# Expert passes of at most 96 rows by strip groups alone, with their slots in reverse, and strip groups behind both row halves in every pass

## The chip, the cores and the metric

One core of one Trainium2 chip runs the whole kernel as one program. The metric is the device time in microseconds of one execution; lower is better. The time before is the median of three runs, 1945.91 us.

## The reference

The kernel computes one residual block for 1024 tokens of width 1024 in float32: a convolution group and a windowed attention group, their output projection, and then a mixture of experts. Only the last part is touched by the change:

```
logits = xf @ router_w + router_b           # 32 experts
top_val, top_idx = lax.top_k(logits, 4)     # 4 experts for each token
gates = softmax(top_val)
h = xb @ w1[e] + b1[e]                      # 1024 -> 2048, rows of one expert
x_glu = minimum(h[:, :1024], 7.0)
x_lin = clip(h[:, 1024:], -7.0, 7.0)
act = x_glu * sigmoid(1.702 * x_glu) * (x_lin + 1.0)
y = act @ w2[e] + b2[e]                     # 1024 -> 1024
out[token] += gate * y
```

Counted from the reference's own routing of its own inputs, the 32 experts get 187, 176, 173, 150, 149, 149, 144, 139, 139, 138, 137, 132, 130 and 129 tokens (14 experts with more than 128), 15 experts get 103 to 128, and three get few: expert 17 gets 77, expert 25 gets 95 and expert 27 gets 75. Expert 0 gets 121.

## The kernel before, in words

The mixed part (convolution, attention, projection, routing) fills the first 425 us. Then follows a loop of passes, one for each expert here, in which the engines run their own loops and meet by semaphores.

**What a pass is.** A pass has 256 slots. The tokens of the expert fill slots 0, 1, 2 and so on, in the order of their ranks (`prep` subtracts a base from the ranks, `one_hots` makes a one-hot matrix of them, `slots_to_tokens` turns it into token numbers on TensorE). The slots behind them get tokens that did not choose the expert, whose gate is exactly 0. All 256 slots are gathered in every pass.

**Tiers.** Each pass is computed for a width n out of `WIDTHS`, the smallest that holds its tokens. The passes are sorted by width, cyclically from the tier of expert 0, by small operations on VectorE just before the loop. Here that gives 18 passes with n = 128, then 3 with 136, 5 with 144, 3 with 152, 2 with 176 and 1 with 192, which is the last.

**TensorE in a pass (`pe_pass`).** The first product has eight blocks m, each of two sides and eight k: 128 matmuls of a 128x128 piece of `w1_sb` (stationary) against n columns of `xT`. The profile shows each float32 matmul as two instructions, so a pass has 256. Block m waits for `hid_free`, the first also for `xt_ev`, the transposed rows: a pass with n = 128 waits for the first half of the slots only (`q4_low`). The second product has slots 0 to 127 as stationary operand, eight pieces for each half of the 1024 columns (`down_rows`, 16 matmuls with 512 columns, 32 instructions), and, in passes of more than 128 rows, the other slots in groups of 32 (`down_quads`). A group uses the array as four strips of 32 columns: each strip takes the same 32 slots against another quarter of the output columns, so a group is 8 x 4 matmuls of 256 columns, 64 instructions. The order is first row half, strip groups, second row half.

**The other engines in a pass.** VectorE adds the bias and clips (`hidden_a`), multiplies (`hidden_b`), ScalarE makes the sigmoid. GpSimd issues eight indirect gathers of the next pass' rows, two behind each of the blocks 4 to 7 of the first product (`gather_quads`), and then the indirect adds of the finished rows into the output (`add_quads` four times where the pass is wide, then `add_rows`); at the head of the next pass it waits until all of these have landed. VectorE transposes the gathered rows into `xT` (eight transposes) when all eight gathers have landed, which fires `xt_ev`; then it adds b2 to what ScalarE has copied out of PSUM: first row half, four strip groups, second row half. The strip groups are copied and biased in every pass, used or not.

**The weights.** There is one buffer for `w1` and one for `w2`. SyncE's loop issues for the next pass: each half of w1 (two transfers of 2048 KB) when blocks 3 and 7 of the first product are done, the first half of w2 (2048 KB) when the first row half and the strip groups are done, the second when the second row half is done, then b2.

```
            if n == P:
                pe.sem_inc(yq_mm, QUADS)
            else:
                down_quads(-(-(n - P) // QG_ROWS))
```

Of the kernel before, what the change touches and what calls it, by code (L numbers as in the profile page):

```python
# [18 lines left out]
P = 128  # L19
# [14 lines left out]
WIDTHS = [128, 136, 144, 152, 176, 192, 256]  # L34
QG_ROWS = 32
# [11 lines left out]
def hybrid_block(nc, x, norm1_g, w_in, conv_w, conv_b, conv_ln_g, conv_ln_b, q_norm_g, k_norm_g, sinks,  # L47
# [11 lines left out]
    with ExitStack() as ctx:  # L59
# [115 lines left out]
        given = sb("given", [P, P])  # L175
        least = sb("least", [P, P])
# [124 lines left out]
        def _(sp):  # L301
# [69 lines left out]
            with sp.Fori(1, n_pass) as q:  # L371
# [61 lines left out]
        def _(pool):  # L433
# [95 lines left out]
            with pool.Fori(0, n_pass) as q:  # L529
# [7 lines left out]
                q_quads = pool.snap(q * QUADS)  # L537
                with pool.If(over > 0):
# [11 lines left out]
        def act_pass(a, q):  # L550
# [22 lines left out]
            take_rows(0)  # L573
            take_quads()
            take_rows(1)
# [241 lines left out]
        def dve_pass(v, q, e, e_next, prep, one_hots):  # L817
# [80 lines left out]
            add_b2(0)  # L898
            q_quads = v.snap(q * QUADS + QUADS)
# [4 lines left out]
            add_b2(1).then_inc(y_ready, 1)  # L904

        @block.vector
        def _(v):
# [43 lines left out]
            link(v.tensor_scalar(tc[:, 1:2], qcol[:], tc[:, 0:1], float(SLOTS // NE), ALU.subtract, ALU.mult))  # L951
# [186 lines left out]
            def prep(ranks, base):  # L1138
                return v.tensor_scalar(r8[:], ranks, base, None, ALU.subtract)
# [23 lines left out]
            link(v.tensor_scalar(tier, left, float(WIDTHS[0]), None, ALU.is_gt))  # L1163
            for n in WIDTHS[1:-1]:
# [5 lines left out]
            link(v.tensor_scalar(keys, circ, 0.0, float(len(WIDTHS)), ALU.is_lt, ALU.mult))  # L1170
# [12 lines left out]
            link(v.tensor_scalar(t1(TIER), t1(WRAP), float(len(WIDTHS)), -float(len(WIDTHS)), ALU.is_ge, ALU.mult))  # L1183
            link(v.tensor_tensor(t1(TIER), t1(TIER), t1(WRAP), ALU.add))
            link(v.tensor_scalar(place[:], iota_c[:, 0:TQ], t1(AT), None, ALU.is_equal))
# [11 lines left out]
            v.tensor_copy(baseB[:], bank[1][:, 3 * TQ:4 * TQ])  # L1197
# [18 lines left out]
        def pe_pass(pe, q, n, halves, slots_to_tokens):  # L1216
# [4 lines left out]
            for m in range(MT):  # L1221
# [12 lines left out]
                if m == 1:  # L1234
                    slots_to_tokens(q + 2, halves)
# [449 lines left out]
```

## Time and profile before

| | |
|---|---|
| median of 3 runs | 1945.91 us (1942.98 to 1947.94) |
| the profiled execution's own time | 1941.44 us |
| its span, first to last instruction | 1939.6 us |
| TensorE (PE) busy | 1904.7 us, 98% of the span |
| weight loads (PEld) busy | 1442.8 us, 74% |
| VectorE (DVE) busy | 1023.9 us, 53% |
| mean granted TensorE clock | 0.996 |
| moved by DMA | 517.28 MB, mean 267 GB/s |

Everything is counted from one profiled execution, in microseconds from the start of its span. PE is TensorE's matmuls, PEld its weight loads, which run beside matmuls, DVE is VectorE, ACT ScalarE, POOL GpSimd, SPq the queue of SyncE. L1230 is line 1230 of the kernel before. A row of a timeline is a group of like instructions: start, time to the end of the last, engine, line, operation, and in brackets the idle time before it and what ended it. The ends of matmuls are modelled, so lengths here are taken from start to start.

### The profile page before, as it was taken

Reading aid. Unit: us, or ns where it says so; the run is one execution under the profiler, and the core shown is the slowest. Engines: PE = TensorE matmul, PEld = TensorE weight load, DVE = VectorE, ACT = ScalarE, POOL = GpSimd, SP = SyncE. Lnnn points to the kernel's source line nnn. Section 1 sums busy time; section 2 is a strip of 40 time slices with the busy share of each in tenths; the row PEclk is TensorE's granted clock in tenths of the full one; section 3 lists DMA queues with packets and bytes.
Section 4 is the critical chain, followed back from the end, with each engine's and each line's share of the span. In section 5 each row is a group of like instructions: output and inputs, shape, how many; then the busy total and the mean of one; then the engine's idle time right before and its main releaser. Section 6 shows DMA issues by size and latency. Waiting matters only on the chain.

```text
span 1939.6 us, 34852 instructions
## 1 busy us (share of the span) xinstructions
PE 1904.7 (98%) x12360; PEld 1442.8 (74%) x12361; DVE 1023.9 (53%) x2829; ACT 439.3 (23%) x966; POOL 455.7 (23%) x434
## 2 busy tenths in 40 slices
PE   8999999989999999999999999999999999999997
PEld 5555554468887778888877888888888888888874
DVE  5999973365555455555545555444444444443332
ACT  4367583121111111111111111111111111110110
POOL 3110110011222112112221211333333333322223
PEclk9999999999999999999999999999999999999999
DMA  7000226358999999999999999999999998887762
GB/s 249 1 1 1 71 60 247 107 184 309 347 354 339 354 354 353 346 338 355 350 343 354 354 348 348 321 319 319 319 319 317 310 311 307 300 299 262 235 215 47
DMA packets 248770, 517.28 MB, mean 267 GB/s; under 512 B 13265, under 2 KB 29165, under 8 KB 248720
## 3 DMA queue, kind: packets, MB, share of 16 engines
q1 hardware_dynamic: 223392, 453.50, 64.8%
q0 software_dynamic: 25312, 63.08, 12.5%
q8 instruction: 35, 0.57, 0.1%
q14 instruction: 15, 0.12, 0.0%
q10 hardware_dynamic: 16, 0.00, 0.0%
HBM read 483.49 MB, written 33.05 MB: 266 GB/s over the span
## 4 chain that ended last, share of the span: by engine, by line
PE 93%; DVE 4%; ACT 1%; DMA 1%; issue 1%; POOL 1%; POOLq 0%; DVEq 0%
PE bank L1230 51%; PE bank L1247 23%; PE bank L1445 6%; PE bank L1321 4%; PE bank L1261 3%; DVE arena L974 2%; PE bank L1357 2%; PE bank L1367 1%; PE bank L1395 1%; PE bank L1615 0%; PE bank L1419 0%; PE bank L1548 0%; PE bank L1404 0%; POOL rs L445 0%; DMA arena<-token_rows,idx_next 0%
## 5 line engine op out<-in xcount | busy, mean ns | idle before, releaser
L1230 PE MATMUL bank<-arena 128*128 128x128 f32 (+5 forms) x8192 | 997.8, 283 | 2.0 <-issue 2.0
L1230 PEld LDWEIGHTS bank<-arena 128*128 128x128 f32 x8192 | 985.9, 191 | 16.9 <-issue 16.9
L1247 PE MATMUL bank<-arena 128*128 128x512 f32 x1024 | 448.5, 594 | 0.0
L419 POOL DMA_INDIRECT arena<-token_rows,idx_q x256 | 248.4, 970 | 709.9 <-PE bank L1230 661.2
L1247 PEld LDWEIGHTS bank<-arena 128*128 128x128 f32 x1024 | 191.2, 190 | 228.7 <-issue 228.7
L835 DVE TENSOR_SCALAR arena<-bank,b1c 128x256 f32<-128x256 f32 x256 | 123.5, 483 | 402.0 <-PE bank L1230 393.4
L556 ACT ACTIVATE arena<-arena 128x256 f32<-128x256 f32 x256 | 106.7, 417 | 860.4 <-DVE arena L835 860.4
L883 DVE STREAM_TRANSPOSE arena<-arena 128x256 f32<-128x256 f32 x256 | 87.3, 408 | 196.9 <-DMA arena<-token_rows,idx_q 196.9
L974 DVE SCALAR_TENSOR_TENSOR arena<-arena,cols 128x512 f32<-128x512 f32 (+1 forms) x226 | 182.3, 807 | 12.8 <-ACT arena L622 5.8
L428 POOL DMA_INDIRECT out<-arena,idxq_cur x56 | 91.3, 1631 | 165.8 <-DVE arena L902 153.3
L847 DVE SCALAR_TENSOR_TENSOR arena<-arena 128x256 f32<-128x256 f32 x256 | 108.8, 425 | 38.0 <-DVE arena L844 9.9
L564 ACT ACTIVATE arena<-bank,gate_cur 128x512 f32<-128x512 f32 x64 | 44.0, 687 | 352.4 <-PE bank L1247 352.4
L837 DVE TENSOR_SCALAR arena<-bank,b1c 128x256 f32<-128x256 f32 x256 | 121.5, 474 | 0.0
L1445 PE MATMUL bank<-arena 128*128 128x512 f32 x256 | 115.6, 599 | 0.8 <-ACT arena L693 0.8
L1321 PE MATMUL bank<-arena 128*128 128x512 f32 x256 | 113.2, 595 | 0.3 <-DVE arena L925 0.3
L844 DVE TENSOR_TENSOR arena<-arena 128x256 f32<-128x256 f32 x256 | 107.3, 419 | 2.9
L424 POOL DMA_INDIRECT out<-arena,idx_cur x32 | 51.3, 1603 | 241.3 <-DVE arena L896 237.6
L896 DVE SCALAR_TENSOR_TENSOR arena<-arena,gate_cur 128x512 f32<-128x512 f32 x64 | 48.1, 752 | 86.1 <-ACT arena L564 74.9
L1321 PEld LDWEIGHTS bank<-arena 128*128 128x128 f32 x256 | 47.5, 190 | 55.0 <-issue 54.6
L1445 PEld LDWEIGHTS bank<-arena 128*128 128x128 f32 x256 | 46.8, 190 | 52.7 <-issue 52.6
L444 POOL TENSOR_SCALAR ss<-ss 128x1 f32<-128x1 f32 (+1 forms) x24 | 10.0, 417 | 271.4 <-DVE ss L987 156.1
L1261 PE MATMUL bank<-arena 128*32 128x256 f32 x1088 | 61.6, 380 | 0.0
(235 smaller groups left out, 1103.6 us busy)
## 6 DMA issues: line engine op xcount, KB each, us to landing
arena<-in_w SPq DMA_DIRECT2D x192, 2048.0 KB, 13.7
arena<-in_b SPq DMA_DIRECT2D x32, 512.0 KB, 13.3
arena<-in_x SPq DMA_DIRECT2D x16, 512.0 KB, 5.4
token_rows<-arena SPq DMA_DIRECT2D x8, 576.0 KB, 3.2
out<-arena SPq DMA_DIRECT2D x8, 512.0 KB, 5.7
arena<-in_b SPq DMA_DIRECT2D x128, 32.0 KB, 11.9
arena<-token_rows,idx_q POOLq DMA_INDIRECT x256
arena<-in_w_in SPq DMA_DIRECT2D x2, 1536.0 KB, 10.8
```

The source lines that it names most:

```text
L419: pool.indirect_dma_start(out=gath_q[:, g, :], out_offset=None, in_=quads_d, in_offset=bass.IndirectOffsetOnAxis(ap=idx_q[:, g:g + 1], axis=0)
L556: a.activation(sg[:, m % 2, :], g1[:, m % 2, :], ACT.Sigmoid, scale=ALPHA).then_inc(sg_ready, 1)
L835: v.tensor_scalar(g1[:, r, :], bank[r][:, 0:SLOTS], b1c[:, m:m + 1], LIMIT, ALU.add, ALU.min).then_inc(g1_ready, 1)
L837: v.tensor_scalar(l1[:, r, :], bank[r][:, SLOTS:], b1c[:, MT + m:MT + m + 1], LIMIT + 1.0, ALU.add, ALU.min).then_inc(hid_free, 1)
L844: v.tensor_tensor(tt[:, r, :], g1[:, r, :], sg[:, r, :], ALU.mult).then_inc(dve_loop, 1)
L847: v.scalar_tensor_tensor(act[:, m, :], l1[:, r, :], 1.0 - LIMIT, tt[:, r, :], ALU.max, ALU.mult).then_inc(act_ready, 1)
L974: link(v.scalar_tensor_tensor(out_, zT[:, c, lo + j:lo + j + n], col(CW + c * WIDTH + j), out_, ALU.mult, ALU.add))
L1230: last = mm(bank[m % 2][:, side * SLOTS:side * SLOTS + n], w1_sb[:, k, lo:lo + P], xT[:, k, 0:n], start=k == 0, stop=k == KD - 1)
L1247: last = mm(bank[4 + b][:], act[:, m, 0:P], w2_sb[:, m, b * HALF:(b + 1) * HALF], start=m == 0, stop=m == MT - 1)
L1261: last = mm(dst[j * QG_ROWS:(j + 1) * QG_ROWS, at:at + D // 4], act[:, m, lo:lo + QG_ROWS], w2_sb[:, m, j * (D // 4):(j + 1) * (D // 4)], ...
L1321: last = mm(dst[:], w_cv[:, k, lo:lo + P], uT[:, k, h * HALF:(h + 1) * HALF], start=k == 0, stop=k == KD - 1)
L1445: last = mm(bank[mixed_bank(t) + b][:], src, w_o[:, k, b * HALF:(b + 1) * HALF], start=part_ == 0 and i == 0, stop=part_ == 1 and i == CT - 1)
```

## The change

- A new tier `FEW`: a pass of at most 96 rows (but for expert 0's) is computed with n = 96. It sorts behind 256, so the three such passes come last, behind the one of 192.
- In these passes the slots are reversed: rank r goes to slot 255 - r. `prep` multiplies by a sign of the pass (`turned`), and the base table carries the flag. The rows then stand in slots 160 to 255: the first product takes `xT[:, k, 160:256]`, the second product runs strip groups 1, 2 and 3 alone, and no row half. Such a pass waits for the transposes of all slots, and both parts of w2.
- In all passes the strip groups follow both row halves: on TensorE, ScalarE, VectorE (add of b2) and GpSimd (the adds into the output). Both halves of w2 wait for the strip groups, and the load of b2 for VectorE's last strip group.
- `hidden_a(0)` moves ahead of `prep` and `one_hots` on VectorE, and `slots_to_tokens` from behind block 1 to behind block 2.
- Passes with n = 96 find the tokens of both slot halves (16 small matmul instructions), those with n = 128 mostly those of one.

```diff
+FEW = 96
+FOLD = 2048
+TIERS = len(WIDTHS) + 1
...
                 for c in range(2):
                     sp.wait_ge(yt_mm, q * 2 + (c - 1))
-                    if c == 0:
-                        sp.wait_ge(yq_mm, q * QUADS)
+                    sp.wait_ge(yq_mm, q * QUADS)
                     load_w2(sp, c, e)
                 sp.wait_ge(y_ready, q)
+                sp.wait_ge(yq_ready, q * QUADS)
                 load_b2(sp, e)
...
+                pool.wait_ge(y_ready, q + 1)
+                pool.sem_inc(pool_past, 1)
+                add_rows(pool)
                 with pool.If(over > 0):
                     for g in range(QUADS):
                         pool.wait_ge(yq_ready, q_quads + g + 1)
                         pool.sem_inc(pool_past, 1)
                         add_quads(pool, g)
                     pool.reg_add(wide, wide, 1)
-                pool.wait_ge(y_ready, q + 1)
-                pool.sem_inc(pool_past, 1)
-                add_rows(pool)
...
             take_rows(0)
+            take_rows(1)
             take_quads()
-            take_rows(1)
...
-            link(prep(rank[:, :, ds(e_next, 1)].rearrange("p t o -> p (t o)"), baseB[:, ds(q + 1, 1)]))
+            hidden_a(0)
+            link(prep(rank[:, :, ds(e_next, 1)].rearrange("p t o -> p (t o)"), baseB[:, ds(q + 1, 1)],
+                      turned[:, ds(q + 1, 1)]))
             one_hots()
-            hidden_a(0)
...
             add_b2(0)
+            add_b2(1).then_inc(y_ready, 1)
             q_quads = v.snap(q * QUADS + QUADS)
             for g in range(QUADS):
...
-            add_b2(1).then_inc(y_ready, 1)
...
-                return v.tensor_scalar(r8[:], ranks, base, None, ALU.subtract)
+                return v.tensor_scalar(r8[:], ranks, base, sign, ALU.subtract, ALU.mult)
...
+            link(v.tensor_scalar(turned[:], bank[1][:, 3 * TQ:4 * TQ], 0.0, None, ALU.is_gt))
+            link(v.tensor_scalar(baseB[:], bank[1][:, 3 * TQ:4 * TQ], -float(FOLD), None, ALU.mult))
+            link(v.scalar_tensor_tensor(baseB[:], turned[:], float(FOLD + SLOTS - 1), baseB[:], ALU.mult, ALU.add))
+            link(v.tensor_scalar(turned[:], turned[:], -2.0, 1.0, ALU.mult, ALU.add))
             v.sem_inc(hid_free, 2)
...
+            at = SLOTS - n if n < P else 0
...
-                            pe.wait_ge(xt_ev, q4 if n > P else q4_low)
-                        last = mm(bank[m % 2][:, side * SLOTS:side * SLOTS + n],
-                                  w1_sb[:, k, lo:lo + P], xT[:, k, 0:n],
+                            pe.wait_ge(xt_ev, q4_low if n == P else q4)
+                        last = mm(bank[m % 2][:, side * SLOTS + at:side * SLOTS + at + n],
+                                  w1_sb[:, k, lo:lo + P], xT[:, k, at:at + n],
                                   start=k == 0, stop=k == KD - 1)
                 last.then_inc(hid_mm, 1)
-                if m == 1:
+                if m == 2:
                     slots_to_tokens(q + 2, halves)
...
-            down_rows(0)
             if n == P:
                 pe.sem_inc(yq_mm, QUADS)
+            if n >= P:
+                down_rows(0)
+                down_rows(1)
             else:
-                down_quads(-(-(n - P) // QG_ROWS))
-            down_rows(1)
+                pe.wait_ge(w2_in[0], q16)
+                pe.sem_inc(yt_mm, 2)
+            if n != P:
+                down_quads(range((SLOTS - n) // QG_ROWS - QUADS, QUADS) if n < P else range(-(-(n - P) // QG_ROWS)))
...
-                for i, n in enumerate(WIDTHS):
+                for i, n in enumerate(WIDTHS + [FEW]):
```

On TensorE, the second product of a pass of 136 rows before (L1230 is the first product, L1247 a row half, L1261 a strip group):

```order
L1230 MATMUL bank<-arena 128x136 x16
L1242 ISA
L1243 REGISTER_ALU
L1247 MATMUL bank<-arena 128x512 x8
L1261 MATMUL bank<-arena 32x256 x32
L1247 MATMUL bank<-arena 128x512 x8
```

And a pass of the new tier on TensorE in the changed kernel (L1241 is the first product, L1276 a strip group; no row half is left):

```order
L1241 MATMUL bank<-arena 128x96 x16
L1286 ISA
L1276 MATMUL bank<-arena 32x256 x32
L1269 REGISTER_ALU
L1276 MATMUL bank<-arena 32x256 x32
L1269 REGISTER_ALU
L1276 MATMUL bank<-arena 32x256 x32
```

Between blocks of the first product and the three strip groups stands nothing else; in the passes of 128 rows and more both L1258 row halves now stand together, with the strip groups behind them.

On GpSimd, the end of the loop before (L419 gathers, L428 adds of strip groups, L424 adds of row halves):

```order
L419 DMA arena<-token_rows,idx_q 128x288 x2
L538 COMPARE_AND_BRANCH
L540 ISA
L428 DMA out<-arena,idxq_cur 4096x256
L540 REGISTER_ALU
L428 DMA out<-arena,idxq_cur 4096x256
L540 REGISTER_ALU
L428 DMA out<-arena,idxq_cur 4096x256
L540 REGISTER_ALU
L428 DMA out<-arena,idxq_cur 4096x256
L543 REGISTER_ALU
L424 DMA out<-arena,idx_cur 1024x1024
```

And in the changed kernel:

```order
L423 DMA arena<-token_rows,idx_q 128x288 x2
L428 DMA out<-arena,idx_cur 1024x1024
L545 COMPARE_AND_BRANCH
L547 ISA
L432 DMA out<-arena,idxq_cur 4096x256
L547 REGISTER_ALU
L432 DMA out<-arena,idxq_cur 4096x256
```

The add of the rows (512 KB) now goes first, and the four adds of strip groups come last; a pass of the new tier issues all five.

## Rows read from the trace of the kernel before

**Rows 1.** The page: busy time of each engine, and the chain that ended last by line.

```profile
PE 1904.7 (98%) x12360; PEld 1442.8 (74%) x12361; DVE 1023.9 (53%) x2829; ACT 439.3 (23%) x966; POOL 455.7 (23%) x434
PE bank L1230 51%; PE bank L1247 23%; PE bank L1445 6%; PE bank L1321 4%; PE bank L1261 3%; DVE arena L974 2%; PE bank L1357 2%; PE bank L1367 1%; PE bank L1395 1%; PE bank L1615 0%; PE bank L1419 0%; PE bank L1548 0%; PE bank L1404 0%; POOL rs L445 0%; DMA arena<-token_rows,idx_next 0%
```

**Rows 2.** Windows, one pass each (128, 128, 144 rows): length, busy times, clock, DMA share, GB/s.

```profile
597.43:640.26 42.83, 42.83 (x299) 35.16 (x298) 23.08 (x74) 7.45 (x15) 9.26 (x9) 1.00 0.99 348
1154.20:1197.23 43.03, 43.03 (x307) 35.36 (x306) 22.00 (x69) 7.45 (x15) 9.26 (x9) 1.00 0.98 347
1340.88:1390.48 49.60, 49.60 (x372) 40.02 (x371) 22.48 (x70) 7.56 (x15) 16.21 (x14) 1.00 0.92 313
```

**Rows 3.** Timeline of PE, a pass of 128 rows: last four blocks, then second product.

```profile
612.15 14.54 PE L1230 MATMUL bank<-arena 128*128 128x128 f32 x128
626.53 13.90 PE L1247 MATMUL bank<-arena 128*128 128x512 f32 x32
```

**Rows 4.** Timeline of PE, wide passes of 136, 152 and 176 rows.

```profile
1212.68 15.07 PE L1230 MATMUL bank<-arena 128*128 128x136 f32 x128
1227.59 7.03 PE L1247 MATMUL bank<-arena 128*128 128x512 f32 x16
1234.55 3.66 PE L1261 MATMUL bank<-arena 128*32 128x256 f32 x64
...
1606.00 16.78 PE L1230 MATMUL bank<-arena 128*128 128x152 f32 x128
1622.62 7.03 PE L1247 MATMUL bank<-arena 128*128 128x512 f32 x16
...
1788.59 7.11 PE L1261 MATMUL bank<-arena 128*32 128x256 f32 x128
```

**Rows 5.** Timeline of PEld: weight loads whose matmuls have one column.

```profile
286.85 0.86 PEld L1470 LDWEIGHTS bank<-ones_ln,arena 128*128 128x128 f32 x7 [0.24 <-issue]
```

**Rows 6.** Timelines of POOL, DVE and PE: last gather of a pass, then the transposes.

```profile
628.84 0.95 POOL L419 DMA_INDIRECT arena<-token_rows,idx_q  x1 [0.30 <-issue]
...
634.95 2.73 DVE L883 STREAM_TRANSPOSE arena<-arena 128x256 f32<-128x256 f32 x8 [6.15 <-DMA arena<-token_rows,idx_q]
...
1781.63 7.03 PE L1247 MATMUL bank<-arena 128*128 128x512 f32 x16
1791.10 2.73 DVE L883 STREAM_TRANSPOSE arena<-arena 128x256 f32<-128x256 f32 x8 [7.30 <-DMA arena<-token_rows,idx_q]
```

**Rows 7.** The queue of SyncE (w2 L290, w1 L285), and the page's time to landing.

```profile
633.73 7.23 SPq L290 DMA_DIRECT2D arena<-in_w  x2
...
655.17 15.68 SPq L285 DMA_DIRECT2D arena<-in_w  x4
arena<-in_w SPq DMA_DIRECT2D x192, 2048.0 KB, 13.7
```

**Rows 8.** Timeline of the last pass, from the end of its first product.

```profile
1904.79 7.03 PE L1247 MATMUL bank<-arena 128*128 128x512 f32 x16
...
1909.88 2.73 DVE L883 STREAM_TRANSPOSE arena<-arena 128x256 f32<-128x256 f32 x8 [2.93 <-DMA arena<-token_rows,idx_q]
1913.27 0.75 DVE L896 SCALAR_TENSOR_TENSOR arena<-arena,gate_cur 128x512 f32<-128x512 f32 x1 [0.35 <-DVEq L890]
1922.64 1.55 POOL L428 DMA_INDIRECT out<-arena,idxq_cur  x1 [0.30 <-issue]
1924.50 1.55 POOL L428 DMA_INDIRECT out<-arena,idxq_cur  x1 [0.30 <-issue]
...
1926.69 0.75 DVE L896 SCALAR_TENSOR_TENSOR arena<-arena,gate_cur 128x512 f32<-128x512 f32 x1 [5.97 <-ACT arena L564]
1928.23 1.55 POOL L424 DMA_INDIRECT out<-arena,idx_cur  x1 [2.18 <-DVE arena L896]
```

**Rows 9.** Windows behind the last adds: columns as in rows 2.

```profile
1926.00:1928.40 2.40, 0.00 (x0) 0.00 (x0) 0.75 (x1) 0.65 (x1) 0.22 (x2) 1.00 0.53 56
...
1934.80:1939.60 4.80, 0.00 (x0) 0.00 (x0) 0.00 (x0) 0.00 (x0) 0.00 (x0) 0.50 0.00 0
```

More of the change, by code:

```diff
@@ L175, in hybrid_block @@
         given = sb("given", [P, P])
+        turned = sb("turned", [P, TQ])
         least = sb("least", [P, P])
@@ L950, in _ @@
             link(v.tensor_reduce(tc[:, 0:1], lg[:], AX.X, ALU.add))
-            link(v.tensor_scalar(tc[:, 1:2], qcol[:], tc[:, 0:1], float(SLOTS // NE), ALU.subtract, ALU.mult))
+            link(v.tensor_scalar(tc[:, 1:2], qcol[:], tc[:, 0:1], float(SLOTS // NE) / FOLD, ALU.subtract, ALU.mult))
+            link(v.memset(cand[:, 1, 0:1], 0.0))
             v.tensor_scalar(rtok[:], tokid[:], float(SEQ - 1), None, ALU.subtract)
@@ L1136, in _, with prep @@
             first_one_hots(NT - 1, NT).then_inc(oh_ready, 1)
-            def prep(ranks, base):
-                return v.tensor_scalar(r8[:], ranks, base, None, ALU.subtract)
+            def prep(ranks, base, sign):
+                return v.tensor_scalar(r8[:], ranks, base, sign, ALU.subtract, ALU.mult)
             def one_hots():
@@ L1162, in _ @@
                                  given[:].rearrange("p (j e) -> p j e", j=ROUNDS), ALU.subtract))
-            link(v.tensor_scalar(tier, left, float(WIDTHS[0]), None, ALU.is_gt))
-            for n in WIDTHS[1:-1]:
+            link(v.tensor_scalar(tier[:, 1:], left[:, 1:], float(FEW), float(TIERS - 1), ALU.is_le, ALU.mult))
+            for n in WIDTHS[:-1]:
                 link(v.scalar_tensor_tensor(tier, left, float(n), tier, ALU.is_gt, ALU.add))
@@ L1169, in _ @@
             link(v.tensor_scalar(circ, tier, tier[:, 0:1], None, ALU.subtract))
-            link(v.tensor_scalar(keys, circ, 0.0, float(len(WIDTHS)), ALU.is_lt, ALU.mult))
+            link(v.tensor_scalar(keys, circ, 0.0, float(TIERS), ALU.is_lt, ALU.mult))
             v.tensor_reduce(wraps[:], keys, AX.X, ALU.max)
@@ L1182, in _ @@
             link(v.scalar_tensor_tensor(t1(PACK), t1(WRAP), float(P), t1(RUN), ALU.mult, ALU.add))
-            link(v.tensor_scalar(t1(TIER), t1(WRAP), float(len(WIDTHS)), -float(len(WIDTHS)), ALU.is_ge, ALU.mult))
+            link(v.tensor_scalar(t1(TIER), t1(WRAP), float(TIERS), -float(TIERS), ALU.is_ge, ALU.mult))
             link(v.tensor_tensor(t1(TIER), t1(TIER), t1(WRAP), ALU.add))
+            link(v.scalar_tensor_tensor(t1(BASE), t1(TIER), float(TIERS - 1), t1(BASE), ALU.is_equal, ALU.subtract))
             link(v.tensor_scalar(place[:], iota_c[:, 0:TQ], t1(AT), None, ALU.is_equal))
@@ L1253, in down_quads @@
                 pe.wait_ge(yq_ev, q * QUADS + QUADS)
-                for g in range(groups):
+                if groups[0] > 0:
+                    pe.sem_inc(yq_mm, groups[0])
+                for g in groups:
                     if g >= 2:
@@ L1259, in down_quads @@
                     for m in range(MT):
+                        if n < P and g == groups[0]:
+                            pe.wait_ge(act_ready, q8 + m + 1)
                         for j in range(4):
@@ L1262, in down_quads @@
                                       w2_sb[:, m, j * (D // 4):(j + 1) * (D // 4)], start=m == 0, stop=m == MT - 1)
-                    last.then_inc(yq_mm, 1 if g < groups - 1 else QUADS - groups + 1)
-            down_rows(0)
+                    last.then_inc(yq_mm, 1 if g < groups[-1] else QUADS - groups[-1])
             if n == P:
                 pe.sem_inc(yq_mm, QUADS)
-            else:
-                down_quads(-(-(n - P) // QG_ROWS))
-            down_rows(1)
+            if n >= P:
+                down_rows(0)
+                down_rows(1)
+            else:
+                pe.wait_ge(w2_in[0], q16)
+                pe.sem_inc(yt_mm, 2)
+            if n != P:
+                down_quads(range((SLOTS - n) // QG_ROWS - QUADS, QUADS) if n < P else range(-(-(n - P) // QG_ROWS)))
         @block.tensor
@@ L1644, in _ @@
             with pe.Fori(0, n_laps) as lap:
-                lap_base = pe.snap(lap * (len(WIDTHS) * P))
+                lap_base = pe.snap(lap * (TIERS * P))
                 def passes(begin, end, n, halves):
@@ L1658, in _ @@
                         length = pe.snap(entry - i * P, min_val=1, max_val=QMAX)
-                        if n > P:
+                        if n != P:
                             passes(0, length, n, 2)
```

1 line of the change is left out of this document (removed).

## The prediction

> **What bounds the kernel now.** The page comes first: TensorE is busy for 98% of the span, and the first and second product of the passes (L1230, L1247, L1261) make up 77% of the chain that ended last [rows 1]. The windows of single passes say the same more sharply: a pass of 128 rows lasts 42.83 us and TensorE is busy for all of it, at the full clock of 2.4 GHz [rows 2]. So a pass costs what TensorE needs, as long as nothing is late. But the DMA share of that pass is 0.99: the 16 engines are nearly full. A pass of 144 rows, which also issues the four adds of strip groups, keeps them busy for 0.92 x 49.60 = 45.6 us, against 0.99 x 42.83 = 42.4 us [rows 2]. The question is therefore not only what TensorE saves in the three small passes, but which of gathers, weights and final adds is late next. All sums are against the profiled execution's own time, 1941.44 us (span 1939.6); it lies 4.5 us below the median of 1945.91, to which I carry the difference over.
>
> **First product with 96 columns in place of 128: saves nothing.** From start to start, 128 instructions take 16.62 us with 152 columns and 14.91 us with 136 [rows 4], so 129.8 and 116.5 ns each, or 0.83 ns per column. On that line 128 columns would take 109.8 ns. They take 14.38 us / 128 = 112.3 ns [rows 3]: the line has already bent. Where the matmuls have one column only, seven weight loads in a row take 0.86 us with 0.19 us for the last, so they start (0.86 - 0.19) / 6 = 112 ns apart [rows 5]. The two numbers agree: below some 131 columns an instruction costs its weight load, 112 ns, whatever its columns. I take 112.3 ns for 96 columns; the other end is the line, 83 ns. A pass has 256 of them, so the saving is between 0 and 256 x (112.3 - 83) = 7.5 us, and I take 0, by the row with one column.
> The Trainium skill ("TensorE: Matmul & The Clock Gate", section on LDWEIGHTS) gives a weight load P / 1.2 ns, with P its columns, which is 107 ns for 128 and speaks against this part of the change; the trace agrees, with 112 ns. By the same page's formula for the gap between isolated matmuls, N / 2.4 + 2.5 ns for each pass over the columns, the saving would be near the upper end.
> Start to second product therefore stays what it is in a pass that finds both slot halves: 43.03 - 13.73 = 29.30 us [rows 2], where 13.73 = 640.26 - 626.53 is the second product of 128 rows [rows 2, 3]. The sixteen small matmuls are in it; most passes of 128 rows have eight, 0.20 us less.
>
> **Second product by three strip groups.** One group takes 3.66 us and two take 7.11 us [rows 4], so a further one adds 3.45 us, and three take 10.56 us. TensorE itself saves 13.73 - 10.56 = 3.2 us.
>
> **What is late next: the transposes.** A pass of the new tier may start only when all slots of its rows are transposed. In a pass of 128 rows the last gather is issued at 628.84, and the eight transposes run from 634.95 to 637.68, which is 11.15 us behind the end of the first product (626.53) [rows 3, 6]. In a pass of 176 rows it is 1791.10 + 2.73 - 1781.63 = 12.20 us [rows 6]. Today 13.73 us of second product and more cover that. The change leaves 10.56 us, and this cover is gone: TensorE waits. I take 11.7 us, between the two, with 0.2 us for the hand-over: 11.9 us. The lower bound is the strips' own 10.6 us, the upper 12.4 us. A small pass with another behind it lasts 29.30 + 11.9 = 41.2 us.
>
> **The transfers.** Both halves of w2 now wait for the end of the strips, and all five adds run beside them. Before, the second half was issued at about 641 and took 13.7 us to land, so at 655 it was in; it was needed at 669 [rows 7]. In the first small pass both halves go out at its start; my estimate is that they are in after some 20 us, of the 29.3 us until the second product. Each small pass asks for 45.6 us of DMA and lasts 41.2 us, so the queue falls 4.4 us behind per pass: 20, 24, 29 us against 29.3. With three passes it just closes. Price 0, bounds 0 and the rival below.
>
> **The last pass.** Now a pass of 192 rows ends the kernel, 1939.60 - 1904.79 = 34.8 us behind its first product [rows 8, 9]. In the changed kernel a small pass does. Counted from E, the end of its first product: the transposes end at E + 7.8 (1909.88 + 2.73 - 1904.79), since few transfers are left, and the first add of b2 starts at E + 8.5 [rows 8]. The second half is now right behind it, so the rows are ready at E + 10. GpSimd takes 0.8 us to react (1927.44 to 1928.23), issues the add of the rows until E + 12.3 and then the four adds of strip groups at 1.86 us each (1924.50 - 1922.64) [rows 8], until E + 19.8. The strips themselves are done at E + 10.6 and hide under that. What follows the last issue: the last add of a strip group was issued until 1926.05, and DMA, busy for 0.53 of the 2.4 us from 1926.00, was still by 1928.40: 2.35 us at most. The add of the rows was issued until 1929.78, and the last 4.8 us, from 1934.80, move nothing: 5 us at most [rows 8, 9]. So the end is at E + 19.8 + 2.3 + 4.8 = E + 27, with bounds of 26 and 29.5 us, the upper with the 5 us of a row add. TensorE's own saving of the last pass is lost here: five adds in a row replace it.
>
> **The other parts, at nothing.** In passes of 128 rows ScalarE and VectorE now do the unused strip groups behind the second row half; VectorE is some 1.3 us later into the next pass, but `hidden_a(0)` no longer waits for the one-hots, so the blocks get their buffers as before; if that cover were gone, block 2 would start late, 1 us in each of 15 passes. In wide passes strips and rows are the same instructions with as many changes of shape: 0, with bounds of -0.1 and +0.1 us in each of 14. Behind the second product w2 comes later, by 7 us, and still has 10 us of slack. Some six small operations before the loop: 0.2 us, bounds 0 and 1.
>
> **The sum.**
> - three passes of 128 rows go: -3 x 42.83 = -128.5
> - the pass of 192 rows is no longer last: its second product, 13.73 + 7.11 + 0.1 = 20.9 in place of 34.8: -13.9
> - two small passes: +2 x 41.2 = +82.4
> - the last small pass: 29.3 + 27.0 = +56.3
> - before the loop: +0.2
>
> Together -3.5 us: 1937.9 for the profiled execution, **1942.4 us** against the median. The bounds of the waits and of the end put it between -7 and +1. A measurement of this kernel can tell 0.3%, 5.8 us; this is less.
>
> **The rivals.**
> - *Columns count* (0.05). If an instruction with 96 columns costs 83 ns, a pass loses 7.5 us more on TensorE, but then the transfers bind: the last pass starts its second product about 6 us earlier, not 22. -9.5 us, 1936.4. Against it stands the row with one column.
> - *Gathers arrive early* (0.14). In the last pass they took until E + 5.1 to arrive, not E + 8.4 [rows 6, 8]. If so in the small passes too, the strips' 10.6 us bind, and two passes are 1.3 us shorter: -6.1 us, 1939.8, just faster. Against it: the DMA engines are full there, as in passes of 128 rows.
> - *The weights fall behind* (0.09), the case that ends slower. If the DMA queue binds from the first small pass, each lasts its 45.6 us of transfers and some 1.5 us in which w1 waits for block 3: 47.1 us in place of 41.2, two times, +11.8, and with -3.5 that is +8.3 us: 1954.2. It decides when w2 of the first small pass lands later than 25 us into it, for then w1 of the third is late too. For it: 0.99 and 45.6 us. Against it: the wide pass ahead leaves the queue empty.
> - *The tier stays empty* (0.01): the counts exclude it. Then 1946.
>
> **How the numbers follow.** The forecast has 0.71; of it 0.05 falls beyond -5.8 us by the spread of three runs. Faster: 0.05 + 0.14 + 0.05 = 0.24. Slower: 0.08, nearly all of the third rival. Within 0.3%: 0.68. The range takes the terms' bounds, the spread of the runs, and the near side of the weights' case, where waits cost a few us: 1937.0 to 1949.5.
>
> **What would show it right or wrong.** L1241 with 96 columns at 112 ns per instruction; the small passes at 41.2 us, with TensorE idle for 1 to 1.5 us at the first instruction of the next, released by VectorE's transposes (L888); L1276 three groups in 10.6 us; GpSimd's last add ending 9 us behind the last matmul, and 27 us from E to the end of the span. Passes of 128 rows must still last 42.83 us. A wait for w1 or w2 in the small passes, or 83 ns, would make it wrong.

## The result, and the profile after the change

| | before | changed |
|---|---|---|
| median of 20 runs each | 1943.83 us (1941.06 to 1947.94) | 1947.51 us (1942.48 to 1950.31) |
| ratio to before, 95% interval | | 1.0016 [1.0009, 1.0023] |
| span of the profiled execution | 1939.6 us | 1945.0 us |
| TensorE matmuls, busy | 12360, 1904.7 us | 12864, 1903.8 us |

I had forecast 3.5 us less. The change costs 0.16%, some 3 us more: below the 0.3% that I called no change, but the interval lies wholly above 1. The forecast of 1942.4 us was counted from 1945.91 us, the median of three runs; counted from the 1943.83 us of twenty it would be 1940.3. TensorE is busy for 1 us less, as the page of the changed kernel shows beside [rows 1]; the page's rows of the first product, of the row halves and of the strips follow:

```profile
PE 1903.8 (98%) x12864; PEld 1454.0 (75%) x12865; DVE 1025.9 (53%) x2835; ACT 439.5 (23%) x966; POOL 480.1 (25%) x446
...
L1241 PE MATMUL bank<-arena 128*128 128x128 f32 (+6 forms) x8192 | 1002.6, 284 | 8.5 <-issue 8.3
...
L1258 PE MATMUL bank<-arena 128*128 128x512 f32 x928 | 403.0, 592 | 0.0
...
L1276 PE MATMUL bank<-arena 128*32 128x256 f32 x1664 | 94.7, 380 | 0.1
```

TensorE was idle for 8.3 us ahead of first products, released by "issue": it waited for nothing that the profile shows. Of these, 1.8 us lie ahead of the very first pass, where the kernel before has 2.0. The timeline of PE tells where the others are (start, length, then the idle time ahead in brackets): the step to the pass of 192 rows, the end of that pass and all of the small ones.

```profile
1736.70 15.86 PE L1241 MATMUL bank<-arena 128*128 128x192 f32 x96 [0.55 <-issue]
...
1779.11 13.90 PE L1258 MATMUL bank<-arena 128*128 128x512 f32 x32
1792.94 7.11 PE L1276 MATMUL bank<-arena 128*32 128x256 f32 x128
1805.93 14.28 PE L1241 MATMUL bank<-arena 128*128 128x96 f32 x96 [5.88 <-issue]
...
1824.25 14.51 PE L1241 MATMUL bank<-arena 128*128 128x96 f32 x128
...
1850.07 10.96 PE L1241 MATMUL bank<-arena 128*128 128x96 f32 x96 [0.20 <-DVE arena L888]
...
1890.45 10.96 PE L1241 MATMUL bank<-arena 128*128 128x96 f32 x96
...
1919.88 10.93 PE L1276 MATMUL bank<-arena 128*32 128x256 f32 x192
```

The 5.88 us lie between the last strip of the 192 pass and the first instruction of the first small pass. The 96 instructions behind it take 14.28 us; in the next two passes they take 10.96. The windows say why (columns as in rows 2, the clock behind POOL's busy time):

```profile
1800.00:1802.00 2.00, 0.05 (x4) 0.00 (x0) 1.27 (x3) 1.86 (x4) 0.23 (x2) 1.00 1.11 161
1802.00:1804.00 2.00, 0.00 (x0) 0.00 (x0) 0.18 (x1) 0.62 (x1) 1.70 (x2) 0.67 0.79 247
...
1806.00:1808.00 2.00, 2.00 (x10) 2.00 (x10) 0.00 (x0) 0.00 (x0) 1.18 (x1) 0.50 1.07 317
1808.00:1810.00 2.00, 2.00 (x11) 2.00 (x11) 0.00 (x0) 0.00 (x0) 0.00 (x0) 0.50 1.11 301
...
1812.00:1815.00 3.00, 3.00 (x25) 3.00 (x24) 1.86 (x7) 0.42 (x1) 0.00 (x0) 0.85 1.05 401
```

During the idle time the granted clock fell to half (1.2 GHz), and it came back only behind 1812. So one hole costs twice: 5.88 us of idle and 14.28 - 10.96 = 3.3 us of half clock, 9.2 us together.

Set against the sum of the prediction, from the first pass of 128 rows to the end (1939.6 - 426.02 = 1513.6 us before, 1945.0 - 428.20 = 1516.8 after):

| part | predicted | measured |
|---|---|---|
| three passes of 128 rows go | -128.5 | -128.5 |
| passes of 136 to 192 rows, up to the end of the last one's first product | 0 | +0.6 |
| 192 pass, end of first product to next start | 20.9 in place of 34.8 | 26.8 in place of 34.8 |
| first small pass | 41.2 | 44.1 |
| second small pass | 41.2 | 40.4 |
| last: first product, then E to the end | 29.3 + 27.0 | 29.4 + 25.1 |
| sum | -3.7 | +3.2 |

The profiled spans differ by 5.4 us instead. The other 2.2 us lie in the first 300 us, in code that the change leaves alone: the eight transposes of 64x64 there start at 295.19 us before and at 297.36 after. In the ten further kernels of the experiments they start between 294.88 (e7) and 300.85 us (e6), in either kind. From them to the first pass it is 130.83 us before and 130.84 after, so the operations added there cost nothing.

### The profile page after: what moved, and what is told of

Same layout as the page of the kernel before. It is cut to its first block and busy times, and to the rows that moved or that the text cites. A ratio compares the mean times of both kernels' runs of the same rounds, so it can differ in the third digit from the quotient of the medians.

```text
span 1945.0 us, 35972 instructions
## 1 busy us (share of the span) xinstructions
PE 1903.8 (98%) x12864; PEld 1454.0 (75%) x12865; DVE 1025.9 (53%) x2835; ACT 439.5 (23%) x966; POOL 480.1 (25%) x446
## 5 line engine op out<-in xcount | busy, mean ns | idle before, releaser
L1241 PE MATMUL bank<-arena 128*128 128x128 f32 (+6 forms) x8192 | 1002.6, 284 | 8.5 <-issue 8.3
L1241 PEld LDWEIGHTS bank<-arena 128*128 128x128 f32 x8192 | 987.9, 192 | 22.5 <-issue 21.4
L1258 PE MATMUL bank<-arena 128*128 128x512 f32 x928 | 403.0, 592 | 0.0
L1258 PEld LDWEIGHTS bank<-arena 128*128 128x128 f32 x928 | 174.3, 190 | 208.1 <-issue 208.1
L428 POOL DMA_INDIRECT out<-arena,idx_cur x32 | 56.0, 1749 | 410.2 <-DVE arena L901 366.6
L432 POOL DMA_INDIRECT out<-arena,idxq_cur x68 | 108.8, 1600 | 41.9 <-DVE arena L908 26.4
L1464 PE MATMUL bank<-arena 128*128 128x512 f32 x256 | 115.6, 599 | 0.8 <-ACT arena L697 0.8
L1340 PE MATMUL bank<-arena 128*128 128x512 f32 x256 | 114.9, 602 | 0.3 <-DVE arena L930 0.3
L1276 PE MATMUL bank<-arena 128*32 128x256 f32 x1664 | 94.7, 380 | 0.1
L1340 PEld LDWEIGHTS bank<-arena 128*128 128x128 f32 x256 | 48.1, 192 | 56.1 <-issue 55.7
L1276 PEld LDWEIGHTS bank<-arena 128*32 128x32 f32 x1664 | 58.2, 110 | 39.3 <-issue 12.1
L1464 PEld LDWEIGHTS bank<-arena 128*128 128x128 f32 x256 | 46.8, 190 | 52.7 <-issue 52.6
```

The lines of the kernel that those rows point to most:

```text
L432: pool.indirect_dma_start(out=out_q, out_offset=bass.IndirectOffsetOnAxis(ap=idxq_cur[:, g:g + 1], axis=0), in_=ytq[:, g, :], in_offset=No ...
L1241: last = mm(bank[m % 2][:, side * SLOTS + at:side * SLOTS + at + n], w1_sb[:, k, lo:lo + P], xT[:, k, at:at + n], start=k == 0, stop=k == ...
L1258: last = mm(bank[4 + b][:], act[:, m, 0:P], w2_sb[:, m, b * HALF:(b + 1) * HALF], start=m == 0, stop=m == MT - 1)
L1276: last = mm(dst[j * QG_ROWS:(j + 1) * QG_ROWS, at:at + D // 4], act[:, m, lo:lo + QG_ROWS], w2_sb[:, m, j * (D // 4):(j + 1) * (D // 4)], ...
L1340: last = mm(dst[:], w_cv[:, k, lo:lo + P], uT[:, k, h * HALF:(h + 1) * HALF], start=k == 0, stop=k == KD - 1)
L1464: last = mm(bank[mixed_bank(t) + b][:], src, w_o[:, k, b * HALF:(b + 1) * HALF], start=part_ == 0 and i == 0, stop=part_ == 1 and i == CT - 1)
```

## The experiments

**Theory A**: the hole is an instruction fetch. The code of the tiers stands in the order 128, 136, ... 192, 256, 96, and no pass is of tier 256. To get from the 192 pass to the small one TensorE's sequencer (the part that reads the instructions) jumps over the body of tier 256 (256 + 18 + 32 + 4 x 64 = 562 matmul instructions, as the profile counts them, and their weight loads), and what stands behind it has to be fetched. **Theory B**: the hole is a real wait that the profile doesn't name (the data or weights of the first small pass). **Theory C**: the switch of tier itself costs it, its load of a table entry and its branch, whatever the distance. Beside these stood the question what the order "strips behind both row halves" costs by itself, in all wide passes.

**e1_few_ahead** puts the code of the small tier ahead of tier 256's; the tier numbers 6 and 7 change places.

```
...
-                for i, n in enumerate(WIDTHS + [FEW]):
+                for i, n in enumerate(WIDTHS[:-1] + [FEW, WIDTHS[-1]]):
```

> The code of the new tier stands ahead of the code of tier 256, which no pass uses here; passes, order and arithmetic are those of the changed kernel. Theory A (TensorE's queue has to jump over the unused code of tier 256 on its way to the small passes, and fetches from there): the idle time before the first small pass falls from 5.88 us to under 1 us, the clock stays at full speed in that pass (first three blocks 11.0 us, not 14.28), so 8 to 9 us less than the changed kernel, ratio to before about 0.997. Theory B (the first small pass waits for its data or weights, whatever the code's place): idle time and ratio stay as in the changed kernel, 1.0016. Theory C (the switch of tier itself, its load of a table entry and its branch): idle stays within 1 us of 5.88.

**e2_body256_empty** keeps tier 256's load and branch and leaves out its body, the matmuls of a pass of 256 rows (no pass here has so many), on TensorE.

```
-                        if n != P:
+                        if n == WIDTHS[-1]:
+                            pe.reg_add(done, done, 0)
+                        elif n != P:
```

> The changed kernel with the body of tier 256 left out (no pass uses it here); its load of the table entry and its branch stay. Theory A (distance of the jump, a fetch): idle before the first small pass under 1.5 us, about as in e1, ratio about 0.997. Theory C (two loads and two branches in a row at this switch, whatever the distance): idle stays 4 to 6 us, ratio 1.001 to 1.002.

**e3_order_only** has the new order of strips and rows everywhere and no small tier.

```
-  link(v.tensor_scalar(tier[:, 1:], left[:, 1:], float(FEW), float(TIERS - 1), ALU.is_le, ALU.mult))
+  link(v.tensor_scalar(tier[:, 1:], left[:, 1:], -float(SEQ), float(TIERS - 1), ALU.is_le, ALU.mult))
...
-                for i, n in enumerate(WIDTHS + [FEW]):
+                for i, n in enumerate(WIDTHS):
```

> The changed kernel without the new tier: no pass falls into it, the small experts are passes of 128 rows again, and strip groups still follow both row halves in all passes. If the new order costs nothing, as predicted: ratio 1.000 within 0.001, passes of 128 rows at 42.83 us. If the 3 us of the result come from the order of the adds, the later load of w2 or the operations before the loop: ratio 1.0010 to 1.0020.

Measured, as the ratio to before: e1 0.9982 [0.9973, 0.9991] (1941.28 us), e2 0.9974 [0.9965, 0.9984] (1938.58 us), e3 1.0003 [0.9995, 1.0012] (1944.62 us). The timelines of PE at the start of the first small pass, e1 first, then e2, then e3 from one pass of 176 rows to the next and at its 192 pass:

```profile
1804.85 10.95 PE L1242 MATMUL bank<-arena 128*128 128x96 f32 x96 [0.52 <-issue]
```

```profile
1799.63 10.95 PE L1241 MATMUL bank<-arena 128*128 128x96 f32 x96 [1.43 <-issue]
```

```profile
1799.21 7.11 PE L1276 MATMUL bank<-arena 128*32 128x256 f32 x128
1806.26 14.59 PE L1241 MATMUL bank<-arena 128*128 128x176 f32 x96
...
1866.71 15.86 PE L1241 MATMUL bank<-arena 128*128 128x192 f32 x96 [0.51 <-issue]
```

With either edit only 0.52 and 1.43 us of idle are left, and the half clock is gone (10.95 us). The small pass of e1 has the same work, registers and waits as in the changed kernel, so B falls. In e2 the load and the branch of tier 256 are still passed, and all the idle there is 1.43 us in place of 5.88, so C falls: it is what stands between, not the branch. From the first pass to the end e1 takes 8.8 us less than the changed kernel, as Theory A had it, but its median is only 6.2 us lower, where I had expected 8 to 9. In the profiled executions the difference lies ahead of the passes: e1 needs 131.86 us from the transposes of 64x64 to the first pass, 1.0 more, and reaches these transposes 3.3 us later, at 300.62.

The order by itself costs little: from the first pass to the end e3 takes 1944.3 - 429.75 = 1514.6 us, 1.0 more than before, 0.5 of it the idle ahead of the 192 pass. e3 shows one thing more. Between two passes of the same tier TensorE jumps back to the start of the body, here over 434 matmul instructions and behind strips, and is not idle at all (1806.26, no bracket). So a jump back to code that has just run costs nothing; the hole comes with a jump ahead.

Why then did nothing show at the other steps between tiers? The next pair asked whether a jump alone makes a hole. **e4_before_skip168** is the kernel before with a tier of 168 rows that no pass uses, between 152 and 176; **e5_order_skip168** is e3 with the same tier.

```
-WIDTHS = [128, 136, 144, 152, 176, 192, 256]
+WIDTHS = [128, 136, 144, 152, 168, 176, 192, 256]
```

> The kernel before, with one more tier of 168 rows that no pass uses (153 to 168 tokens occur for no expert). Its code stands between tiers 152 and 176, and TensorE's queue jumps over it. Theory A: TensorE idles for 4 to 6 us before the first pass of 176 rows and then runs it at the half clock for some us: ratio 1.003 to 1.005. Theories B and C: idle under 1 us there, ratio 1.000 to 1.001.

> e3 (new order in all passes, no small passes) with the unused tier of 168 rows between 152 and 176, as in e4. Theory A1 (the jump takes 5 us or more wherever it is, and what stands last in the pass ahead decides how much of it shows: 32 row instructions of 0.43 us hide it in e4, 64 strip instructions of 0.055 us do not): TensorE idles 5 to 7 us before the first pass of 176 rows, and runs at the half clock for some us behind it; ratio 1.003 to 1.005. Theory A2 (only the jump over tier 256 is long, its code being larger, and the order has no part in it): about 1.2 us idle, as in e4; ratio 1.000 to 1.001.

Measured: e4 1.0001 [0.9992, 1.0010] (1944.66 us), e5 1.0058 [1.0043, 1.0072] (1954.61 us). PE's timeline of e4 at the jump, then e5's:

```profile
1735.78 3.66 PE L1261 MATMUL bank<-arena 128*32 128x256 f32 x64
1739.37 7.13 PE L1247 MATMUL bank<-arena 128*128 128x512 f32 x16
1747.70 9.81 PE L1230 MATMUL bank<-arena 128*128 128x176 f32 x64 [1.19 <-issue]
```

```profile
1743.72 3.66 PE L1276 MATMUL bank<-arena 128*32 128x256 f32 x64
1751.94 16.90 PE L1241 MATMUL bank<-arena 128*128 128x176 f32 x96 [4.56 <-issue]
```

The jump is the same. In e4 the pass ends in a row half of 7.13 us, and the hole is 1.19 us; in e5 it ends in strips and the hole is 4.56 us, with half clock behind (16.90 us for what takes 14.59 in the next pass of 176 rows). I had expected 4 to 6 us in e4 as well; that was wrong, and it refined A to **A1**: TensorE's sequencer runs ahead of the array by what is queued. The 16 row matmuls last 7.13 / 16 = 0.45 us each (the expectations of e5 and e6 say 32 of them; the timeline has 16), a strip matmul 3.66 / 64 = 0.057 us. Behind a row half the branch is reached while some us of work still wait, and the fetch lies under them; behind strips little work is queued when the branch is reached. The idle of e5, 4.56 us, is less than the 5 to 7 that A1 was given.

The DMA view bears the fetch out. In e4 the instruction queue (q8) moves a block while the last row half still runs; in the changed kernel the window of 1801 to 1802 has none, and the one of 1802 to 1803, when TensorE is already idle, has this one:

```profile
q8 instruction: 1, 0.02, 5.8%
```

Windows of 0.1 us put that block in its place in all four kernels with such a jump (the last one is e6, below):

| | work ahead ends | block on q8, from | next pass starts | block to start |
|---|---|---|---|---|
| changed kernel, 562 jumped over, behind two strip groups | 1800.05 | 1802.2 | 1805.93 | 3.7 |
| e5, 434, behind one strip group | 1747.38 | 1747.7 | 1751.94 | 4.2 |
| e4, 434, behind a row half | 1746.51 | 1743.9 | 1747.70 | 3.8 |
| e6, 562, behind a row half | 1803.24 | 1800.8 | 1804.50 | 3.7 |

From the block to the next pass it is 3.7 to 4.2 us in each. What differs is when the block moves: 2.2 and 0.3 us behind the end of the work, or 2.4 and 2.6 us ahead of it. At the same step of e1 and e2, without the body between, q8 moves no block from 1794 to 1808 and from 1788 to 1803.

e5's ratio is above the 1.003 to 1.005 that I expected. The jump costs it 4.56 + 2.3 = 6.9 us, and from the first pass to the end its profiled execution takes 1952.4 - 430.69 = 1521.7 us, 7.1 more than e3's. Another 1.0 us lies between the transposes of 64x64 and the first pass (131.88 us against 130.92). The medians are 10 us apart, with four runs of e5; what the remaining 2 us are stays open.

**e6_rows_last** tests the cover in the changed kernel itself. The jump stays where it is; in passes of 136 to 192 rows TensorE does the strips between the two row halves, as before the change.

```
+            between = P < n <= P + 2 * QG_ROWS
+            if between:
+                down_rows(0)
+                down_quads(range(-(-(n - P) // QG_ROWS)))
+                down_rows(1)
-            if n >= P:
+            elif n >= P:
...
-            if n != P:
+            if n != P and not between:
```

> The changed kernel, but in passes of 136 to 192 rows TensorE again does its strip groups between the two row halves; the jump over tier 256 stays. Theory A1: the pass of 192 rows ends with 32 row instructions, 7 us, and the idle time before the first small pass falls from 5.88 us to 1 to 2.5 us, the clock staying up: 7 to 8 us less than the changed kernel, ratio about 0.998. Theory A2: idle stays 5 to 6 us, ratio 1.0015.

**e7_fewer_adds** is e1 in which GpSimd issues only the adds of strip groups 1 to 3 in small passes; the add of the rows and of group 0, whose rows are empty there, are left out.

```
...
-                pool.wait_ge(y_ready, q + 1)
-                pool.sem_inc(pool_past, 1)
-                add_rows(pool)
+                with pool.If(over < TIERS - 2):
+                    pool.wait_ge(y_ready, q + 1)
+                    pool.sem_inc(pool_past, 1)
+                    add_rows(pool)
+                    pool.reg_add(rowed, rowed, 1)
...
-                    for g in range(QUADS):
+                    for g in range(1, QUADS):
```

> e1, in which the small passes issue only the adds of strip groups 1 to 3: their row half and strip group 0 hold slots whose gate is 0, so the output is the same. If GpSimd's five adds in a row set the end, as predicted: two issues of 1.86 us less at the end, 3 to 4 us less than e1, ratio 0.996 to 0.997. If the last strip group is what comes last: 0 to 1 us less.

Measured: e6 0.9977 [0.9967, 0.9986] (1939.77 us), e7 0.9976 [0.9965, 0.9986] (1939.26 us). The timeline of PE of e6 at the jump:

```profile
1789.06 7.11 PE L1276 MATMUL bank<-arena 128*32 128x256 f32 x128
1796.10 7.13 PE L1258 MATMUL bank<-arena 128*128 128x512 f32 x16
1804.50 10.95 PE L1241 MATMUL bank<-arena 128*128 128x96 f32 x96 [1.26 <-issue]
```

The same jump over the same 562 matmuls, with a row half ahead of it: 1.26 us in place of 5.88, and full clock, 8.0 us less from the first pass to the end (1940.6 - 431.82 = 1508.8). That confirms A1 where the time was lost. Behind a row half the idle is the same over 562 instructions as over 434 (1.26 and 1.19 us), so the length of the unused body doesn't show; that strips cost 5.88 us here and 4.56 in e5 goes with two strip groups ahead of the jump in place of one, which was not tried by itself.

In e7 the adds at the end are three instead of five, here in the timeline of its last pass:

```profile
1911.73 11.27 PE L1296 MATMUL bank<-arena 128*32 128x256 f32 x192
...
1921.46 1.27 DVE L927 SCALAR_TENSOR_TENSOR arena<-arena,gq_cur 128x256 f32<-128x256 f32 x3
1923.54 0.49 DVE L927 SCALAR_TENSOR_TENSOR arena<-arena,gq_cur 128x256 f32<-128x256 f32 x1 [0.81 <-ACT arena L594]
1923.84 1.69 POOL L432 DMA_INDIRECT out<-arena,idxq_cur  x1 [9.03 <-issue]
1925.83 1.58 POOL L432 DMA_INDIRECT out<-arena,idxq_cur  x1 [0.30 <-issue]
1927.72 1.56 POOL L432 DMA_INDIRECT out<-arena,idxq_cur  x1 [0.31 <-issue]
```

Two adds less bring 1.8 us (from E, the end of the first product, to the end 1935.1 - 1911.7 = 23.4 us, in e1 1940.5 - 1915.3 = 25.2) and not the 3 to 4 that I expected. The first add starts at E + 12.1, where in e1 the first of five starts at E + 10.7 (1926.06), so 1.4 us are lost there; the last add is followed by 5.8 us in place of 5.1. What holds the first add is not shown: it waits for VectorE's operation on strip group 1, and those on groups 0 to 2 were done by 1922.73, 1.1 us earlier.

**e8_cols32** is e1 with 32 columns in place of 96 in the first product of small passes (the hidden values of the other 64 rows are left out); **e10_cols64** the same with 64 (32 rows left out). The question was whether an instruction below 96 columns is any shorter.

```
-  last = mm(bank[m % 2][:, side * SLOTS + at:side * SLOTS + at + n], w1_sb[:, k, lo:lo + P], xT[:, k, at:at + n],
+  w = 32 if n < P else n
+  last = mm(bank[m % 2][:, side * SLOTS + at:side * SLOTS + at + w], w1_sb[:, k, lo:lo + P], xT[:, k, at:at + w],
```

> e1 with 32 in place of 96 columns in the first product of the small passes; the hidden values of all but 32 slots are then not computed there. If the weight load of 112 ns sets the time of an instruction: 112 to 113 ns each, blocks of the small passes as in e1, span as e1. If columns count (0.83 ns each): 256 instructions save up to 13 us per pass, less what DMA then holds up.

> e1_few_ahead with 64 columns per instruction in the first product of the small passes (the hidden values of the other 32 rows are left out, so the output is not the reference's). Theory N (the half clock of e8_cols32 comes with how few columns TensorE moves per weight load): with 64 columns the granted clock in the small passes lies between, some stretches at half; if it stays full throughout, 112 to 113 ns per instruction and the time of e1_few_ahead within 3 us, and then 64 columns show by themselves that columns below 96 save nothing. Rival (the half clock of e8 was this one execution's): full clock and 112 ns. Rival (columns count at full clock): about 85 ns per instruction in the stretches with full clock.

One run of each: e8 2009.48 us, e10 1940.62 us. The windows of e8 in its first small pass (columns as in rows 2), and the timeline of PE of e10:

```profile
1803.00:1805.00 2.00, 2.00 (x21) 2.00 (x19) 0.92 (x3) 1.62 (x2) 1.08 (x1) 1.00 0.91 170
1806.00:1820.00 14.00, 14.00 (x67) 14.00 (x67) 4.68 (x15) 0.83 (x2) 2.88 (x2) 0.50 1.01 332
1829.00:1855.00 26.00, 26.00 (x124) 26.00 (x123) 6.95 (x22) 1.40 (x4) 6.12 (x6) 0.50 0.57 196
```

```profile
1818.17 14.48 PE L1243 MATMUL bank<-arena 128*128 128x64 f32 x128
1832.58 11.27 PE L1278 MATMUL bank<-arena 128*32 128x256 f32 x192
1843.89 10.93 PE L1243 MATMUL bank<-arena 128*128 128x64 f32 x96
```

From start to start, as the 112.3 ns of [rows 3] were taken, an instruction with 64 columns takes (1832.58 - 1818.17) / 128 = 112.6 ns, and one with 96 columns in the changed kernel (1838.69 - 1824.25) / 128 = 112.8. So a third fewer columns saves nothing, and this part of the prediction is measured by itself. With 32 columns TensorE starts at the full clock. PEld's timeline of e8 has 19 weight loads in the 2.20 us from 1802.59; with 0.19 us for the last they start (2.20 - 0.19) / 18 = 112 ns apart, so again nothing is saved. Then the granted clock falls to half although TensorE is busy without a gap, and an instruction takes 26.00 / 124 = 210 ns. e8 took 68 us more than e1, so it gives no price for the small pass as a whole.

**e9_all_three** joins the edits of e1, e6 and e7.

> The few tier's code ahead of tier 256's (as e1_few_ahead), only three adds per small pass (as e7_fewer_adds), and in passes of 136 to 192 rows TensorE does the strips between the two row halves (as e6_rows_last). Theory A1 (far jump uncovered, rest small): the three gains lie in different places and add: ratio about 0.9970, 0.4 to 1 us below e7's time (e3's new order alone cost 1.0 us, of which 0.5 us idle at the step to 192); idle before the first small pass under 0.3 us. Rival: the gains of e1 and e6 are the same gain (both only take away the idle), so the ratio equals that of e7, 0.9976, with the idle unchanged within 0.5 us.

Measured: 0.9969 [0.9957, 0.9981] (1938.64 us). Its timeline of PE, from the first product of the 192 pass to the first small pass, has no bracket at either step:

```profile
1740.62 15.76 PE L1261 MATMUL bank<-arena 128*128 128x192 f32 x96
...
1789.89 7.11 PE L1296 MATMUL bank<-arena 128*32 128x256 f32 x128
1796.93 7.13 PE L1278 MATMUL bank<-arena 128*128 128x512 f32 x16
1803.90 10.85 PE L1261 MATMUL bank<-arena 128*128 128x96 f32 x96
```

The idle times of 0.5 us at the steps to 192 and to the small tier, which e1 and e7 keep, are gone. From the first pass of 136 rows to the end e9 takes 1937.9 - 1075.37 = 862.5 us, e1 1940.5 - 1075.20 = 865.3: 2.8 us less, of which E to the end gives 1.9 (1937.9 - 1914.6 = 23.3 us against 25.2). It beats both kernels, the changed one by 0.47%. Between e7 and e9 the times themselves can't tell (0.9976 and 0.9969, with intervals that overlap); only the timeline does.

## Why the prediction was wrong

- **The step that failed is the second term of the sum**, "its second product, 13.73 + 7.11 + 0.1 = 20.9 in place of 34.8", together with the sentence that strips and rows are "the same instructions with as many changes of shape: 0". The second product took what it was given, 13.83 + 7.11 us. Behind it stood 5.88 us that no term held: the first step in this kernel that jumps over a tier's unused body, right where the change had taken away the row half that would cover it. I priced instructions and waits, and not the instruction stream. Order of code and order of work each looked like nothing; e1 and e6 show that undoing either one takes nearly all of the cost away (0.52 and 1.26 us of idle are left).
- The hole's second half is the clock: 3.3 us in the first small pass, 44.1 us in place of 41.2.
- Both could have been asked of the code ahead of the run. The Trainium skill ("Runtime: NRT & Kernel Launch", section on instruction fetch mechanics) says that a taken branch whose target isn't in the current window has to fetch it by DMA before execution goes on. The runs agree: the block on q8 moves 3.7 to 4.2 us ahead of the pass behind each such jump, with 5.88 and 4.56 us of idle behind strips and 1.19 and 1.26 behind a row half.
- **First product, 112.3 ns at 96 columns**: right, 112.8 ns, and 112.6 with 64 columns. The rule of the Trainium skill of P / 1.2 ns for a weight load ("TensorE: Matmul & The Clock Gate", section on LDWEIGHTS), 107 ns for 128 columns of weights, came close; its formula for the gap between isolated matmuls, which falls with the columns, did not hold here.
- **Three strip groups** were priced at 10.56 us. From start to start they took 10.95 in the second small pass (1890.45 - 1879.50), and 10.98 and 11.19 in e1: 0.4 to 0.6 more, for which the sum of one group and two held nothing.
- **Transposes late next**: right in kind. In the small pass from 1805.93 they end at E + 11.3 and release the next pass with 0.20 us of idle; in the second they end at E + 10.7 and TensorE finds them done, so the strips set the time. The wait that I put at 1 to 1.5 us was 0.2 and 0: the rival "gathers arrive early" came true in part. The rows of VectorE:

```profile
1847.28 2.73 DVE L888 STREAM_TRANSPOSE arena<-arena 128x256 f32<-128x256 f32 x8 [6.52 <-DMA arena<-token_rows,idx_q]
...
1887.46 2.73 DVE L888 STREAM_TRANSPOSE arena<-arena 128x256 f32<-128x256 f32 x8 [5.84 <-DMA arena<-token_rows,idx_q]
```

- **The last pass**: right but for its last piece. The transposes end at E + 7.8, the first add is issued until E + 12.5 (12.3 forecast) and the last until E + 20.0 (19.8 forecast):

```profile
1924.90 2.73 DVE L888 STREAM_TRANSPOSE arena<-arena 128x256 f32<-128x256 f32 x8 [2.92 <-DMA arena<-token_rows,idx_q]
...
1930.55 1.84 POOL L428 DMA_INDIRECT out<-arena,idx_cur  x1 [7.58 <-DVE arena L908]
...
1938.30 1.55 POOL L432 DMA_INDIRECT out<-arena,idxq_cur  x1 [0.30 <-issue]
```

  From there it is 1945.0 - 1939.85 = 5.2 us to the end, not 2.3 + 4.8 = 7.1. The end is at E + 25.1, below my lower bound of 26. Windows of 0.1 us show DMA moving until 1941.7, 1.8 us behind the last issue, and nothing in the 3.3 us from there to the end: the closing that I had put at 4.8 us was the piece that was too large. Before the change nothing moves from 1934.4 on, 5.2 us; why the closing is shorter now stays open.
- **Passes of 128 rows** stay at 42.8 us, **the operations before the loop** cost nothing (130.83 and 130.84 us), and **the weights** never fell behind: in the small passes TensorE's only idle times are the 5.88 and the 0.20 us above.

Without the hole, the forecast stands within its bounds of -7 to +1: e1, which changes nothing but the place of the code, took 3.66 us less than the kernel before. That this is so near to the 3.5 forecast is luck. From the first pass to the end its trace gives 1940.5 - 432.48 = 1508.0 us, 5.6 less than before where the terms of the sum give 3.7; 1.8 of the difference is the end that I had priced too high. The time of the changed kernel, 1947.51 us, lies within the stated range, but that is luck too: the cause is in none of the rivals, and the range was counted from a median 2.1 us above that of the twenty runs.

## What to carry to other kernels

When a change adds a variant of a loop body, look where its code stands in each engine's instruction stream and what the engine jumps over to reach it; place the variants in the order in which they run. Where a jump over unused code can't be avoided, end the work ahead of it with few long instructions rather than many short ones: here a row half of 7.1 us in place of strips took the idle from 5.88 to 1.26 us. And price an idle time of some us on TensorE with the half clock behind it, here 3.3 us on 5.9.

## What the hardware showed beyond that

- A jump over 562 unused matmul instructions on TensorE costs 5.88 us idle behind strip matmuls of 0.056 us, and 1.26 us behind row matmuls of 0.45 us; over 434 it costs 4.56 and 1.19 us. The block on the instruction queue moves 3.7 to 4.2 us ahead of the next matmul in all four. Other distances were not measured. A jump back over 434 such instructions, to start the same body again, shows no idle (e3).
- Idle times of 5.88 and 4.56 us brought a half clock behind them (3.3 and 2.3 us); those of 1.43, 1.26 and 1.19 us brought none.
- The granted clock fell to half while TensorE was busy without a gap, with f32 matmuls of 32 columns each behind its own weight load (e8: 0.50 from 1806 on, in passes where 64 and 96 columns kept 1.00). At that clock an instruction takes 210 ns in place of 112. It is one run of one kernel.
- The steps between tiers without a jump cost nothing behind one strip group (up to the step to 176 rows) and 0.5 us behind two (the step to 192, and in e1 and e7 the step to the small tier); behind a row half they cost nothing (e9). Why stays open.
